# A two-block model on one core: the second block by token tiles from its attention on

## The reference

```python
h = modulate(x, norm1_g, sh1, sc1)
z = h @ w_in + b_in
q = rmsnorm(z_q); k = rmsnorm(z_k)                    # 8 heads of 64
y_hy = hyena(z_hy) @ w_hy_out
y_na = attend(rope(q), rope(k), v, k_ctx, v_ctx, rpb) @ w_na_out
gate = sigmoid(z_gate)
x = x + g1 * ((gate[..., :1024] * y_hy + gate[..., 1024:] * y_na) @ w_out)
h = modulate(x, norm2_g, sh2, sc2)
# peer: for each token and each of 8 heads
s = (h @ w_q) . keys            # two sets of 128 scores
idx, g = best 16 of the 16 x 16 sums of the two top 16, softmax
x = x + g2 * sum_k g_k * gelu(h . u[idx_k]) * v[idx_k]
```

## Time and profile before

| | us |
|---|---|
| median of three runs | 2702.1 (2698.96 to 2702.61) |
| the profiled execution | 2704.44 |
| its span in the profile | 2702.5 |
| granted TensorE clock, mean | 0.972 of full |
| busy: PE, DVE, ACT, POOL | 2506.6, 2072.8, 1257.6, 271.6 |
| attention turns, from the first transpose | 1879.6 to 1967 |
| w_na and w_out2 | 1967.2 to 2010.6 |
| first gather, last gather | 2034.1, 2655.5 |

### The profile page before, as it was taken

How to read it: one execution, slowest core, us unless ns; L and a number is a source line. 1 busy time by engine, 2 the same in 40 slices (tenths; PEclk the granted TensorE clock), 3 DMA queues, 4 the chain that set the end, 5 groups by cost and what they waited for, 6 DMA issues and landing times. The chain is left out here.

```text
span 2702.5 us, 37397 instructions
## 1 busy us (share of the span) xinstructions
PE 2506.6 (93%) x14282; PEld 2161.1 (80%) x14282; DVE 2072.8 (77%) x3104; ACT 1257.6 (47%) x1540; POOL 271.6 (10%) x290
## 2 busy tenths in 40 slices
PE   5999999999999999999999999989998998778787
PEld 4789997787888888888888877747777898777786
DVE  6778984767898989899898974635748878887875
ACT  3234443236777777677777763103422333323322
POOL 0000001000000000000000000000003444333331
PEclk9999999989999999999999998999989999999999
DMA  8647675557999999999999956211558999999997
GB/s 350 245 176 285 273 286 199 216 197 286 354 356 355 356 346 344 355 353 356 353 358 354 355 190 240 114 42 67 212 236 347 412 421 420 420 421 421 421 421 298
DMA packets 109273, 824.90 MB, mean 305 GB/s; under 512 B 11864, under 2 KB 15192, under 8 KB 16096
## 3 DMA queue, kind: packets, MB, share of 16 engines
q1 hardware_dynamic: 71504, 551.75, 53.5%
q0 software_dynamic: 36864, 268.45, 24.0%
q10 hardware_dynamic: 720, 2.24, 0.2%
HBM read 821.34 MB, written 1.05 MB: 304 GB/s over the span
## 5 line engine op out<-in xcount | busy, mean ns | idle before, releaser
L1682 DVE TENSOR_TENSOR ring_r<-ring,arena_r 128x2048 fp32r<-128x2048 f32 x336 | 770.2, 2292 | 11.5
L2064 ACT ACTIVATE arena_r<-ring 128x2048 fp32r<-128x2048 f32 x378 | 725.6, 1920 | 29.0 <-DMA ring<-in_ffn_w_down 14.4
L634 PE MATMUL ps<-arena_r 128*128 128x512 f32 (+1 forms) x1120 | 417.2, 373 | 1.5 <-DVE arena_r L1718 1.5
L636 PE MATMUL ps<-arena_r 128*128 128x512 f32 x896 | 349.3, 390 | 0.0
L635 PE MATMUL ps<-ring_r,arena_r 128*128 128x512 f32 x896 | 348.6, 389 | 0.0
L1344 PE MATMUL ps<-sel,ring 128*128 128x128 f32 x2096 | 267.9, 285 | 59.7 <-ACT sel L2064 58.5
L1344 PEld LDWEIGHTS ps<-sel,ring 128*128 128x128 f32 x2096 | 251.9, 198 | 73.8 <-ACT sel L2064 71.5
L2064 ACT ACTIVATE sel<-cs,arena 128x128 f32<-128x128 f32 x256 | 102.8, 402 | 420.8 <-DVE arena L2022 381.5
L1344 PE MATMUL ps<-sel,arena 128*128 128x128 f32 x2000 | 249.5, 281 | 43.8 <-ACT sel L2064 38.1
L1344 PEld LDWEIGHTS ps<-sel,arena 128*128 128x128 f32 x2000 | 236.4, 195 | 55.3 <-ACT sel L2064 48.4
L634 PEld LDWEIGHTS ps<-arena_r 128*128 128x128 f32 x1120 | 211.3, 189 | 35.6 <-DVE arena_r L1718 1.8
(11 more groups left out here) (282 smaller groups left out, 3864.0 us busy)
## 6 DMA issues: line engine op xcount, KB each, us to landing
ring<-in_moe_w_gate SPq DMA_DIRECT2D x112, 1024.0 KB, 5.4
ring<-in_moe_w_up SPq DMA_DIRECT2D x112, 1024.0 KB, 5.5
ring<-in_moe_w_down SPq DMA_DIRECT2D x112, 1024.0 KB, 5.2
ring<-in_ada_w SPq DMA_DIRECT2D x24, 1024.0 KB, 9.6
ring<-in_ada_w SPq DMA_DIRECT2D x12, 2048.0 KB, 7.9
ring<-in_w_in SPq DMA_DIRECT2D x10, 2048.0 KB, 10.5
ring<-in_w_ada SPq DMA_DIRECT2D x8, 2048.0 KB, 10.1
ring<-in_ffn_w_gate SPq DMA_DIRECT2D x14, 1024.0 KB, 5.2
```

Of the source, the lines that this page charges most:

```text
L634: e.matmul(out, xs[0], ws[0], start=start, stop=False, skip_group_check=True)
L636: return e.matmul(out, xs[1], ws[0], start=False, stop=stop, skip_group_check=True)
L1682: v(e.tensor_tensor(ring_low[ring.half[unit]], ring.buf[unit], mo.high[unit_at[unit] % NHIGH].bitcast(F32), ALU.subtract), ("low", unit))
L2064: A.mark(e.activation(out, src, func, **kw), name)
```

## The change

- **Order of turns**: all eight heads of tile 0, then all of tile 1. Score matmuls come in pairs of heads that lie in opposite halves of the partitions, 64 deep, straight from k and context k; the padded copies and their zeroing go. One copy for two heads takes the attention's result to SBUF. Scores use banks 0 to 3, transposes bank 4, sums bank 5, all side work banks 6 and 7.
- **Side work of PE**: all four first gate pieces run before the turns; the four w_hy pieces and four gate pieces run two halves a turn in the turns of tile 0; w_na of tile 0 in turns 8 and 9, w_out2 of tile 0 in turns 10 and 11, sums of its norm in turn 12, its spread in turn 15.
- **DVE**: three column dots a turn in turns 0 to 7, then merges, residual and norm of tile 0 in turns 8 to 15. The gate is tanh of half the argument plus one, and the half goes into `half_g1`.
- **Tile 1** after tile 0's first queries and scores: w_na, then after head 1's query w_out2, ahead of row 0 on PE; on DVE the merge stands between head 0's first eight indices and the others, the residual in rows 1 and 2, the norm in rows 8 to 11; head 2's choices start at row 12.
- **Queries** by `JOBS`: heads 0 to 3 for tile 0 and, at rows 81 to 111, for tile 1; heads 4 to 7 for both tiles at once.
- **Places**: w_na in the arena, w_pq's third and fourth tile in the arena after the turns, the key table and half of the bias in one slot. Gathers turn through eight buffers; two more join at 50, 82, 98 and 116, sixteen in all.

The diff, cut to its core (lines with a plus or blank ahead are those of the new kernel):

```diff
-    turn, had, out = deque(range(NOWN + 2)), {}, []
-    joins = {24: (NOWN + 2, NOWN + 3), 58: (NOWN + 4, NOWN + 5), 92: (NOWN + 6, NOWN + 7),
-             96: (NOWN + 8, NOWN + 9)}
+    turn, had, out = deque(range(8)), {}, []
+    joins = {50: (8, 9), 82: (10, 11), 98: (12, 13), 116: (14, 15)}
...
+HEADS = [(t, h) for t in range(2) for h in range(8)]
+JOBS = [*((h, (0,)) for h in range(4)), *((h, (0, 1)) for h in range(4, 8)), *((h, (1,)) for h in range(4))]
+def job_rows():
+    at = {2: (3, 5), 3: (8, 11), **{j: range(16 * j - 48, 16 * j - 35, 4) for j in range(4, 8)},
+          **{j: (9 * j + 9, 9 * j + 12) for j in range(8, 12)}}
+    asked = {r: (j, n) for j, rows in at.items() for n, r in enumerate(rows)}
+    queried = {rows[-1] + len(rows) // 2: j for j, rows in at.items()}
+    return asked, queried, {r + 2: j for r, j in queried.items()}
+ASKED, QUERIED, SCORED = job_rows()
...
         def row_buffer(i):
...
+            place, used = (
+                lambda: (ring.buf["bias", 1], P["attended", 15]),
+                lambda: (at(4096), P["w_na", 1, 1]),
+                lambda: (at(12570), V["merged2", 1, 1]),
+                lambda: (part(("w_out2", 0), 0), P["mix2", 1, 0]),
+                lambda: (part(("w_out2", 0), 1), P["mix2", 1, 0]),
+                lambda: (part(("w_out2", 1), 0), P["mix2", 1, 1]),
+                lambda: (part(("w_out2", 1), 1), P["mix2", 1, 1]),
+                lambda: (at(10522), P["mix2", 1, 1]),
+                lambda: (at(0), P["pq", 5]),
+                lambda: (at(2048), P["pq", 5]),
+                lambda: (at(14618), P["pq", 7]),
+                lambda: (at(16666), P["pq", 7]),
+                lambda: (part(("w_pq", 0), 0), P["pq", 9]),
+                lambda: (part(("w_pq", 0), 1), P["pq", 9]),
+                lambda: (part(("w_pq", 1), 0), P["pq", 11]),
+                lambda: (part(("w_pq", 1), 1), P["pq", 11]))[b]()
+            return place, P["rows", had] if had is not None else used
...
         def sp(e):
...
+            e.wait_ge(*P["hyena done"])
+            e.wait_ge(*V["hyena done"])
+            e.dma_start(na_tile(0), T["w_na"][0]).then_inc(in_na[0], 16)
+            for at, t in ((s[0], ada[4]), (s[1], ada[5])):
+                slot(at)
+                load_ada(t)
+            slot(s[2])
             load(("w_in2", 4608), T["w_in2"][9])
+            e.wait_ge(*V["roped", "k"])
+            e.dma_start(na_tile(1), T["w_na"][1]).then_inc(in_na[0], 16)
+            for at, t in ((s[0], ada[6]), (s[1], ada[7])):
+                slot(at)
                 load_ada(t)
+            for n, at in ((0, s[3]), (1, s[0])):
+                slot(at)
                 load(("w_out2", n), T["w_out2"][n])
+            for n, at in ((0, s[1]), (1, s[2])):
+                slot(at)
                 load(("w_pq", n), T["w_pq"][n])
+            slot(kept)
+            load_half("keys", T["keysT"])
+            e.wait_ge(*P["attended", 15])
+            e.dma_start(pq_tile(2), T["w_pq"][2]).then_inc(in_pq2[0], 16)
+            e.dma_start(pq_tile(3)[:, 0:2048], T["w_pq"][3][:, 0:2048]).then_inc(in_pq3[0], 16)
+            e.wait_ge(*P["w_na", 1, 0])
+            e.dma_start(pq_tile(3)[:, 2048:4096], T["w_pq"][3][:, 2048:4096]).then_inc(in_pq3[0], 16)
...
         def pe(e):
...
+            pieces = [piece(c0, i, 2, hT, "hT x") for c0 in (3072, 3584) for i in range(2)]
+            behind_heads = [branch("w_hy", m.zc, i // 2, i % 2, ASIDE[2:]) for i in range(4)]
+            behind_heads += [piece(c0, i, 2, hT, "hT x", ASIDE[2:]) for c0 in (4096, 4608) for i in range(2)]
...
+            its = head_turns()
 
             def scores(i):
+
+                at = []
+                for j in (i, i + 1):
+                    h, t = its[j]
+                    r = slice(64 * (h % 2), 64 * (h % 2) + 64)
+                    at.append((bank(("score", j), SCORES), r, h // 2, t))
+                for c, k in ((0, m.kn), (256, m.kc)):
+                    for j, (b, r, p, t) in enumerate(at):
+                        last = e.matmul(b[:, c:c + 256], m.qn[r, p, 128 * t:128 * t + 128], k[r, p, :],
+                                        start=True, stop=True)
+                        if c:
+                            P.mark(last, ("score", i + j))
+            e.wait_ge(*V["roped", "k"])
+            e.wait_ge(*V["normed", "kc"])
...
+            first = chain.from_iterable(behind_heads)
+            na0, out0 = na(0), out2(0)
+            for i in range(0, 4, 2):
                 scores(i)
+            some(first, 1)
             for i, (h, t) in enumerate(its):
...
+                b = bank(("turn", i), (4,))
                 e.wait_ge(*V["scaled", i])
                 P.mark(turned(b, [m.pt[i % 2][:, 128 * k:128 * k + 128] for k in range(4)]), ("turn", i))
+                if i % 2 and i + 3 < len(its):
                     scores(i + 3)
+                if t == 0:
+                    some(first, 1)
+                elif i < 10:
+                    some(na0, 1)
+                elif i < 12:
+                    some(out0, 2)
+                elif i == 15:
+                    peer_spread(0)
+                b = bank(("attended", i // 2), (5,)) if i % 2 == 0 else ps.bank["attended", i // 2]
                 e.wait_ge(*A["turn", i])
                 r = slice(64 * (h % 2), 64 * (h % 2) + 64)
                 P.mark(summed(b[r, 0:128], [(m.vs[k][:, 64 * h:64 * h + 64], m.pt[i % 2][:, 128 * k:128 * k + 128])
                                               for k in range(4)]), ("attended", i))
+                if t == 0:
+                    some(first, 1)
+                elif i < 10:
+                    some(na0, 1)
+                elif i < 12:
+                    some(out0, 2)
+                elif i == 12:
+                    peer_sums(0)
...
+            for n in range(2):
+                query(0, n)
+            some(na1, 1)
+            key_scores(0)
+            tokens(0)
+            some(na1, 4)
+            for n in range(2):
+                query(1, n)
             key_scores(1)
+            some(out1, 8)
             for i in range(256):
                 t = i // 128
                 if i % 128 == 0:
                     for q in range(2):
                         bank(("peer", t, q), (2 * t + q,))
+                if i == 5:
+                    peer_sums(1)
+                if i == 9:
+                    peer_spread(1)
+                if i in ASKED:
+                    query(*ASKED[i])
                 if i in SCORED:
                     key_scores(SCORED[i])
+                if i == 123:
+                    tokens(1)
...
         def dve(e):
...
...
+            def merged_na(t, n):
+                c = slice(128 * t, 128 * t + 128)
+                hy, na = se2.gate[:, 4 * n:4 * n + 4, c], se2.gate[:, 8 + 4 * n:12 + 4 * n, c]
+                e.wait_ge(*A["tanh", 2 + n])
+                v(e.scalar_tensor_tensor(na, na, 1.0, v4(taken(("w_na", t, n)), 4), ALU.add, ALU.mult))
+                emptied(("w_na", t, n))
+                v(e.tensor_tensor(hy, hy, na, ALU.add), ("merged2", t, n))
+
+            def added(t, n):
+                c = slice(128 * t, 128 * t + 128)
+                b = v4(taken(("mix2", t, n)), 4)
+                for j in range(4):
+                    k = 4 * n + j
+                    v(e.scalar_tensor_tensor(xT[:, k, c], b[:, j, :], se2.half_g1[:, k:k + 1], xT[:, k, c], ALU.mult,
+                                             ALU.add), ("x", "second", t, n))
+                emptied(("mix2", t, n))
+
...
+            for i in range(16):
                 if i + 2 < 16:
                     peak(i + 2)
+                    if i == 5:
+                        ring.emptied["bias", 0] = V.now
                 if i + 1 < 16:
                     scaled(i + 1)
+                if 1 <= i < 5:
+                    merged_hy(i - 1)
+                if i in (8, 9):
+                    merged_na(0, i - 8)
+                if i in (10, 11):
+                    added(0, i - 10)
+                if i < 8:
+                    some(hidden, 3)
+                if i == 9:
+                    v(e.tensor_scalar(m.half_g1, mod[2][:, 16:24], 0.5, None, ALU.mult))
+                    v(e.scalar_tensor_tensor(pr.scr[:, 2304:2312], mod[2][:, 32:40], 1.0, pvc("norm2_g", 0, 8), ALU.add,
+                                             ALU.mult))
+                if i == 14:
+                    rstd(("norm_peer", 0), pr.scr[:, 2048:2049])
+                if i == 15:
+                    normed(0, range(8))
...
                     yield from experts_of(t, h, 0, 8)
+                    for n in range(2):
+                        merged_na(1, n)
                     next8(m.cand, m.bs, m.bp)
...
+                if i in (1, 2):
+                    added(1, i - 1)
+                if i == 8:
+                    rstd(("norm_peer", 1), m.scr[:, 2049:2050])
+                if i in (10, 11):
+                    normed(1, range(4 * i - 40, 4 * i - 36))
```

(23 more changed lines are left out.)

398 lines of the change are left out of this document (185 added, 213 removed).

## The result

The changed kernel takes 2722.3 us in the median of four runs (2721.5 to 2724.2), the kernel before 2702.4 in four runs beside them. The ratio is 1.0077, 95% interval 1.0065 to 1.0089: **slower by 20 us by the medians and 20.8 by the ratio; the forecast was 2696, with 2712 as the end of its range.**

A forecast was written before the change was run, and what follows sets the result against it. The end was taken as a stream of 256 gathered rows, bound by the first gather's start and VectorE's pace in rows 0 to 96. Sum: -17.9 + 11.5 = -6.4 from 2702.1, say 2696 us; range 2683 to 2712.

The forecast's parts named there:

- part 2: Early rows after the first gather: vector work, waits and fewer buffers make them 11.5 us later.
- Sixteen buffers in the end instead of seventeen: Late rows: one buffer fewer costs nothing, since gathers were then many rows ahead.
- DMA below 400 GB/s until gather 50 and full from then: Gathered rows: a sign that would show the forecast right; 420 GB/s from the start would show B.
- C: Early rows: VectorE's in-order queue waits for w_out2; row 32 over 113 us after first gather, 2709 us; chance 0.24.
- turn 12 starts: Attention loop: summed turn times put turn 12 at 1977.7 us; later than 1985 would show the forecast wrong.
- spread to first gather: From spread of tile 0's factor to first gather: 25 us, against 19.9 in the old kernel.
- first gather earlier by: End of part 1, attention until tile 0 is normed: first gather at about 2016 us, 18 us earlier.
- saved by a score pair: Attention scores: 64-deep matmuls in alternating array halves take half, saving 0.75 us a pair in four pairs, 3 us.
- row 32 behind the first gather: VectorE takes row 32 105.5 us after the first gather, against 95 before.
- early rows, up to 80: Early rows: 10.5 us later by vector work and waits, 13.6 by transfers alone; 11.5 taken.
- forecast A: Whole kernel: the forecast itself, 2696 us, own range 2690 to 2702; chance 0.45.
- Rival D: Score matmuls: ten tile switches cost 3.3 us and the 3.0 of halving goes, 2702 us; chance 0.14.

The follow-up runs named there:

- late: Changed kernel with its four joins moved from gathers 50, 82, 98 and 116 to 54, 88, 106 and 126: 2701.6 us, ratio 0.9999 to the kernel before.
- late_rows: `late` with the 64-row score matmuls of a pair issued half after half instead of alternating halves: ratio 0.9994 to the kernel before.
- late_fewer: `late` with 12 VectorE instructions of tile 1's residual and norm left out: 2697.2 us, ratio 0.9979 to the kernel before.
- late_spread: `late` with queries' copies a row later, Exp behind tile 1's root, and tile 1's spread in row 8 instead of 9: 2697.2 us, ratio 0.9980.
- seven: Changed kernel with no joins and seven row buffers to the end instead of eight: 2718.3 us, ratio 1.0054 to the kernel before.

## Why the prediction was wrong, by its steps

**The step that failed** is in part 2: "Sixteen buffers in the end instead of seventeen: nothing, gathers were then many rows ahead." I counted the buffers and not when they join. The gathers are many rows ahead only as long as POOL issues them, and each join puts a wait for TensorE at the head of POOL's queue, with every later gather behind it. What is queued behind a wait on its own engine I had asked for SP's queue and for VectorE's, and not for POOL's. The numbers were on the table: joins 50, 82, 98, 116, queries at rows 44, 76, 93, 111, and 2.49 us a row from the earlier trace rows. q + b - n gives waits of 5, 10, 17 and 22 us; in the kernel before the joins stood 13 to 16 rows behind their queries. The runs put the price at 21 us: 18 for the last two, 2 to 3 for the first two. Also false was what hung on it, "DMA below 400 GB/s until gather 50 and full from then".

None of my rivals was this mechanism. C had the right sign with another place: row 32 was taken 104.2 us behind the first gather, far from its 113, and VectorE did not wait for w_out2 ahead of row 3. Its own time was 2709, and its sum takes 25 us for row 32 at 118, which is 23 behind the 95 of before. The 2722 measured are above the 2712 at which my range ended.

The other steps stood, with these sizes:

| step | forecast | measured |
|---|---|---|
| turn 12 starts | 1977.7 | 1982.0, or 1980.0 net of the 2.0 ahead |
| spread of tile 0's factor | 1991 | 1995.4, or 1993.4 |
| spread to first gather | 25 | 24.75 |
| first gather earlier by | 18 | 15.9 net of the 2.0; 17.0 in `late`, 16.7 net |
| saved by a score pair | 0.75 | 0.68, or 0.58 with the switch ahead of it |
| row 32 behind the first gather | 105.5 | 104.2 |
| early rows, up to 80 | +11.5 | +12.0, and +12.9 to the end in `late` |
| later joins | 0 | +21.2 behind row 80; +20.3 at row 255 against `late` |
| queries in rows 81 to 111 on TensorE | 0 | 0 but for the joins (`late` runs them at 420 GB/s) |

The start came 2 us less early than forecast, in the first turns, where a projection waited 3.20 us for its bank behind turn 1 (TensorE of the changed kernel):

```profile
1898.62 3.35 PE L684 MATMUL ps<-arena,ring 128*128 128x256 f32 x8 [3.20 <-DVE arena L2052]
```

`late` is the kernel without the join term: 17 us gained and 12.9 lost. Its span is 2698.4 against 2702.5, the 4 us of that sum; timed, it is level with the kernel before (2.7 us faster to 2.2 slower), and the execution of the kernel before that was profiled took 2704.4, longer than its medians. So `late` has the parts of forecast A, and their 6.4 us of gain were 2 too many by the spans and 6 by the times.

**Rival D**: the score pair is the one number that was right for a reason that isn't shown. In the kernel before the four 128-deep products of two turns (two lines of two instructions a turn) took 0.87 a turn, 1.74 a pair:

```profile
1886.13 0.60 PE L1236 MATMUL ps<-arena 128*128 128x256 f32 x2
1886.57 0.59 PE L1237 MATMUL ps<-arena 128*128 128x256 f32 x2
1887.00 1.24 PE L620 MATMUL ps<-arena,ring 128*128 128x256 f32 x5
```

Now a pair takes 1.06 (1891.34 to the next group at 1892.40), 0.53 a head, and not the 0.75 to 0.9 a head that I gave as a sign. I took the halving from alternating halves; `late_rows` alternates less and takes 1.08. Why 64-deep products are quicker in either order is open.

The feared switch does show, as a small cost. TensorE of the changed kernel, the first two pairs together and then two groups of transposes (L692), one ahead of a pair and one ahead of 128-deep products:

```profile
1877.49 2.00 PE L1302 MATMUL ps<-arena 64*128 64x256 f32 x16
1879.41 1.99 PE L684 MATMUL ps<-arena,ring 128*128 128x256 f32 x8
...
1890.81 0.60 PE L692 MATMUL ps<-cs,arena 128*128 128x128 f32 x4
...
1901.81 0.60 PE L692 MATMUL ps<-cs,arena 128*128 128x128 f32 x4
1902.24 1.89 PE L684 MATMUL ps<-arena,ring 128*128 128x256 f32 x8
```

Sixteen instructions take 1.92 us to the next group and eight take 1.06, so eight more are 0.86, 0.107 each, half of the 128-deep 0.218, and 0.20 are left for the way out. A pair starts 0.53 us behind the transposes ahead of it, other products 0.43 or 0.44 in four of six turns: 0.10 for the way in. These 0.3 us a pair are my estimate from the starts. The Trainium skill (TensorEngine Tiling (Array Packing), Key Properties) says that a change of the tiling mode drains the engine; the trace agrees, as far as starts can tell, with about 0.3 us there and back where rival D took 0.33 for each of ten switches and no halving. `late` came out at D's 2702, but not for D's reason: the halving is there.

**The early rows**: I had two readings of 10.5 (vector work and waits) and 13.6 (transfers). `late_fewer` shows that the vector work counts in full, `late_spread` that 4 us more were a chain over engines at tile 1's norm. In the changed kernel that chain hid in VectorE's waits for ScalarE, and removing those alone gave nothing. `seven` shows that the transfers stand close behind.

## What to carry to other kernels

When one engine issues transfers in order, a new buffer is a wait at the head of that queue: place the join no sooner than the releasing row plus the number of buffers already in play, and compute (releasing row + buffers - join) x row time before believing that more buffers cost nothing. That is the wait; its price is at most the part of it in which the DMA has nothing left to move. Ask first whether they are needed: eight here did what sixteen did, and seven cost 14 us. And where a chain runs over four in-order engines, find the short instruction that stands behind long ones on each queue; moving a matmul of 0.39 us ahead of 4.5 us of others gave 4 us, on top of an edit that removed two waits and had given nothing.

## What the runs showed of the hardware that I had not expected

- A hold-up of the gathers' issue of 10.3 us left the DMA idle for 2.6 us, one of 18.7 for 5.7, one of 21.1 for 11.1 and one of 24.2 for 8.5: what was issued before covers the rest.
- Behind the two longest, TensorE issued its matmuls haltingly (busy 4.81 of 12 us), which nothing in the profile explains.
- Between 2154 and 2234 us eight buffers of one row keep the DMA at 418 to 419 GB/s, seven at 391 and 403.
- Eight instructions of 64x256 took 1.06 to 1.08 us up to the next group, whether their halves alternated or not, where eight of 128x256 for the same scores had taken 1.74. About 0.3 us a pair goes to the two changes of depth.
